# The first group of products behind each norm: high-part products ahead of low-part products, with waits of their own

## The reference, cut to what matters

```python
def rms_norm(x, gain):
    y = x * rsqrt(mean(x * x, axis=-1) + 1e-6)
    return y * gain

h = rms_norm(x, gain)
first = h @ w          # the group of products that this change touches
```

## Time and profile before

| What | Value |
|---|---|
| median of 3 runs | 1635.24 us (1633.99 to 1635.32) |
| profiled execution, device time | 1636.7 us |
| span of its profile | 1634.9 us |
| mean granted TensorE clock | 0.994 |
| DMA | 269.63 MB, mean 165 GB/s |

### The profile page before, as it was taken

The page is one execution under the profiler, slowest core; times in us unless marked ns, Lnnn a source line. Parts: engine busy times, 40 slices in busy tenths (PEclk is TensorE's granted clock), DMA queues, the critical chain, the costliest instruction groups (busy, mean ns, idle before and its releaser), DMA issues. The chain is left out here.

```text
span 1634.9 us, 23336 instructions
## 1 busy us (share of the span) xinstructions
PE 1594.5 (98%) x8942; PEld 1375.3 (84%) x8942; DVE 951.6 (58%) x1449; ACT 801.9 (49%) x1352; POOL 165.8 (10%) x187
## 2 busy tenths in 40 slices
PE   7999999999999999999999999999999999999897
PEld 6888899988888887888889988878888879878886
DVE  5555475444765545555456544665554688577865
ACT  6444464445364444444355454454443555453642
POOL 0000022211200000000021221120000301010100
PEclk9999999999999999999999999999999999999998
DMA  7666455343555555655546443446665453255421
GB/s 244 207 201 203 147 177 192 131 142 129 168 174 186 182 191 166 196 188 184 183 143 197 155 129 127 150 152 213 206 207 192 152 181 117 78 170 170 143 70 52
DMA packets 76431, 269.63 MB, mean 165 GB/s; under 512 B 8480, under 2 KB 9504, under 8 KB 76320
## 3 DMA queue, kind: packets, MB, share of 16 engines
q1 hardware_dynamic: 76320, 268.14, 49.9%
HBM read 267.06 MB, written 1.05 MB: 164 GB/s over the span
## 5 line engine op out<-in xcount | busy, mean ns | idle before, releaser
L289 DVE TENSOR_TENSOR wlo<-raw,whi 128x1024 fp32r<-128x1024 f32 (+4 forms) x468 | 564.9, 1214 | 414.4 <-ACT whi L283 371.2
L283 ACT ACTIVATE whi<-raw 128x1024 fp32r<-128x1024 f32 (+3 forms) x496 | 508.5, 1034 | 433.2 <-PE bank L339 408.3
L337 PE MATMUL bank<-whi,hh 128*128 128x512 f32 (+4 forms) x1312 | 497.8, 379 | 6.8 <-DVE hl L373 3.7
L339 PE MATMUL bank<-whi,hl 128*128 128x512 f32 (+4 forms) x1312 | 486.4, 371 | 0.0
L338 PE MATMUL bank<-wlo,hh 128*128 128x512 f32 (+4 forms) x1312 | 485.8, 370 | 0.0
L337 PEld LDWEIGHTS bank<-whi,hh 128*128 128x128 f32 x1312 | 248.1, 189 | 49.7 <-DVE hl L373 7.0
L339 PEld LDWEIGHTS bank<-whi,hl 128*128 128x128 f32 x1312 | 247.8, 189 | 40.3
L338 PEld LDWEIGHTS bank<-wlo,hh 128*128 128x128 f32 x1312 | 248.3, 189 | 37.3
L337 PE MATMUL bank<-hh,whi 128*128 128x256 f32 x480 | 142.1, 296 | 0.0
L339 PE MATMUL bank<-whi,gl 128*128 128x512 f32 x352 | 138.7, 394 | 0.0
L338 PE MATMUL bank<-wlo,gh 128*128 128x512 f32 x352 | 137.9, 392 | 0.0
(11 more groups left out here) (295 smaller groups left out, 1672.3 us busy)
## 6 DMA issues: line engine op xcount, KB each, us to landing
raw<-W SPq DMA_DIRECT2D x464, 512.0 KB, 3.3
raw<-W SPq DMA_DIRECT2D x26, 384.0 KB, 3.5
raw<-W SPq DMA_DIRECT2D x8, 416.0 KB, 3.0
tab<-tab SPq DMA_DIRECT2D x6, 384.0 KB, 3.9
raw<-W SPq DMA_DIRECT2D x4, 426.0 KB, 3.1
raw<-W SPq DMA_DIRECT2D x6, 192.0 KB, 2.8
x<-x_in SPq DMA_DIRECT2D x2, 512.0 KB, 5.8
tab<-gains SPq DMA_DIRECT2D x2, 512.0 KB, 4.3
```

The lines of the kernel that those rows point to most:

```text
L283: high = act.op(lambda e: e.activation(whi[i][:, 0:w], r[:, 0:w], ACT.Copy), self.landed[c], free)
L289: tok = (low or dve).op(lambda e: e.tensor_tensor(wlo[i][:, 0:w], r[:, 0:w], whi[i][:, 0:w].bitcast(F), ALU.subtract), self.landed[c], hig ...
L337: pe.op(lambda e: e.matmul(dst, ah, bh, start=start, stop=False), *tokens, mark=False)
L339: return pe.op(lambda e: e.matmul(dst, al, bh, start=False, stop=stop), mark=mark)
```

## The change

In a call with a norm, each held chunk is now issued in two passes. The first pass issues, for both k-tiles of the chunk, the two matmuls that read `hh`. The second issues the one that reads `hl`. The first pass waits for the chunk's weights and for a new token, the last ACT operation that wrote `hh` of that half; the second waits for the last `hl`. Number, form and operands of the matmuls stay the same, as do all programs of ACT, DVE, POOL and SP. Only the order of PE's matmuls inside a chunk of these eight groups and PE's waits differ.

```diff
@@ row_group
             k = 0
+            first = norm
             while k < nk:
@@
-                        for kk in range(k0, k0 + n):
+                        if first:
+                            dst, tsl = got[t][1][:, 0:w], slice(t * 128, (t + 1) * 128)
+                            for kk in range(k0, k0 + n):
+                                ws = slice((kk - k0) * w, (kk - k0 + 1) * w)
+                                mm(dst, hh[:, kk, tsl], ch[:, ws], kk == 0, False, ready, first.high[t, kk // 4],
+                                   got[t][2])
+                                mm(dst, hh[:, kk, tsl], cl[:, ws], False, False)
+                            for kk in range(k0, k0 + n):
+                                ws = slice((kk - k0) * w, (kk - k0 + 1) * w)
+                                tok = mm(dst, hl[:, kk, tsl], ch[:, ws], False, kk == nk - 1, first.ready[t, kk // 4],
+                                         mark=(kk == k0 + n - 1))
+                        for kk in range(k0, k0 + n) if not first else ():
                             j = kk - k0
                             tok = mm3(got[t][1][:, 0:w], [p[:, kk, t * 128:(t + 1) * 128] for p in a],
@@
-                hold = 1
+                hold, first = 1, None
                 yield
@@ Norm
+                self.high = {}
@@ Norm.turn
-                self.ready[t, n] = low
+                self.high[t, n], self.ready[t, n] = high, low
```

## The result

| | before | after |
|---|---|---|
| median | 1635.24 us | 1630.98 us (1629.26 to 1632.83, 13 runs) |
| profiled execution, device time | 1636.7 us | 1630.93 us |
| span of its profile | 1634.9 us | 1629.1 us |

The ratio to the kernel before, run beside it, is 0.9971, with a 95% interval of 0.9963 to 0.9980: 4.7 us less (3.3 to 6.0). The forecast was 1629.5 us, 5.7 us less. Direction, mechanism and range were right; the size was 1.0 us too large in the ratio.

The account below looks back on a forecast made before the run. PE, busy 98% of the span, was taken to bound the kernel. Stalls of 5.9 us removed less 0.2 added gave 5.7 us less, from the median 1635.24 to 1629.5 us; range 1627.6 to 1632.9.

Parts of the forecast that it names:

- The bound and the place: PE, busy 98% of the span, bounds the kernel; L337's loads wait for `hl` in eight places, 7.0 us in all.
- The loss per place: At row tile 1's first matmul after eight norms: 0.62, 0.86 and 0.84 us in three places, 5.9 us in all.
- The restart of 0.11: After a stall at 512 columns the next matmul comes 0.34 us behind instead of 0.23, another 0.11 lost.
- What the change adds: A small stall stays in the two first mixers, 0.2 us together; 32 more waits on loads, taken at 0.
- Exactly when `hl` is there: At 416 columns, row tile 1's fifth matmul falls at 207.90; its load wants to begin 0.19 sooner, costing 0 to 0.30.
- The bound of 0.30 each: Upper bound per new wait on a load: bare load of 0.19 plus restart of 0.11, 9.6 us in all.
- Does the gain come through?: Behind each place the weights' chain must keep up; in the first place its slack falls from 3.0 to 2.2 us.
- half of it swallowed: Rival: work begun before the stall (squares, row factor, queued loads) keeps its time, half the gain goes, 1632.4; chance 0.12.
- Nothing happens: Rival: the first pass still waits on DVE behind `hl`, the stall stands, 1635.2; chance 0.04.
- the new waits cost: Rival: each of 32 new waits keeps its load from being hidden, 0.30 each, 9.6 us, giving 1639.1; chance 0.03.
- The clock's stretches: Rival: late phases meet one half-clock stretch more or less, at most 3.4 us, giving 1632.9 or 1626.1; chance 0.06 both ways.
- the seven microseconds of the earlier trace: The 7 us behind 1568, with the clock at 0.51 and 24 PE matmuls, said to cost at most 3.4 us.

Follow-up runs that it names:

- row tile 0 alone: The kernel before, with the two-pass order and split waits for row tile 0 only, row tile 1 issued as before: 1635.70 us, ratio 1.0002.
- the two kernels with one row tile each: The kernel before with the change in one row tile only: row tile 1 gave 1631.25 us, ratio 0.9968; row tile 0 gave 1635.70 us, ratio 1.0002.
- the kernel with the waits alone: The kernel before, its matmul order kept, with the change's split waits: 1635.12 us, ratio 0.9993; run again 1633.18 us, ratio 0.9984.
- the kernel with the order alone: The change's matmul order on the kernel before, the first pass still waiting for `hl`: 1634.96 us, ratio 0.9997.

## Why the prediction was right, and where not

**The bound and the place.** PE is still busy for 98%, and up to 1341 us the path moved by under 0.2 us anywhere else than in the places and at the broadcast. Right.

**The loss per place** (0.62, 0.86 and 0.84 in the three shown, 5.9 in all from one row of the waits). Measured 5.73 won and 2 x 0.10 left, so 5.9. Right to a tenth. The restart of 0.11 was a real part of it: it is 0.9 us of the 5.9.

**What the change adds.** "Exactly when `hl` is there" at 416 columns: the fifth matmul started in its slot and cost the 0.10 that I took. Elsewhere nothing. The 32 new waits were taken at 0. With row tile 0 alone, the twelve within the path cost 0.1 us at most. The bound of 0.30 each was far off.

**Does the gain come through?** This is the step that failed, by 0.64 us. I looked at the weights' chain behind the first place and found 3.0 us of slack, which held: no new wait for weights appeared. I didn't look at the row factor's chain behind each place, which I had named only in a rival. PE itself needs the row factor in four of the eight places, the mixers, where it is broadcast. In three of them PE comes late enough (0.14 us from the first transpose to the next product, before and after). In the seventh place the norm has two gains, `spreads` has a longer chain of small steps, DVE slows them, and PE was already waiting. The mechanism was that of "half of it swallowed": work begun before the stall doesn't move. It took 0.64 of the 5.7, one place whole, not half of all. With it the sum is 5.7 - 0.6 = 5.1 us, and 1630.1 from the median; measured 4.7, interval 3.3 to 6.0, and 1630.98. What is left is smaller than the runs can tell.

**Nothing happens** and **the new waits cost** are excluded by the two kernels with one row tile each, and by the waits table.

**The clock's stretches** did fall otherwise. The price was about right, the framing was not: it is not one stretch more or less behind this change, but three to five in every trace between 1290 and 1610 us, in several patterns, and two traces of one and the same kernel can differ in theirs. Windows of the kernel with the waits alone, and of the kernel before, over the same stretch of time (columns as in the earlier trace rows):

```profile
1388.00:1393.50 5.50, 5.50 (x39) 4.98 (x38) 2.54 (x5) 2.76 (x7) 0.00 (x0) 1.00 0.31 100
1393.50:1397.00 3.50, 3.50 (x14) 3.01 (x14) 1.69 (x8) 0.43 (x2) 0.00 (x0) 0.52 0.00 0
```

```profile
1388.00:1393.50 5.50, 5.50 (x35) 4.75 (x33) 4.99 (x11) 2.62 (x9) 0.00 (x0) 1.00 0.02 4
1393.50:1397.00 3.50, 3.50 (x31) 3.42 (x31) 0.60 (x4) 0.43 (x1) 0.00 (x0) 1.00 0.45 150
```

And the seven microseconds of the earlier trace rows in the kernel with the order alone, whose path is that of before, with a stretch of its own earlier:

```profile
1517.00:1520.40 3.40, 3.40 (x19) 3.40 (x18) 2.91 (x4) 3.38 (x12) 0.00 (x0) 0.50 0.68 233
1568.00:1575.00 7.00, 7.00 (x44) 6.23 (x44) 3.86 (x10) 2.46 (x6) 0.00 (x0) 1.00 0.13 50
```

In the same 7 us PE ran 24 matmuls before and 44 here, and the path moved by 3.2 us, against the 3.4 of the prediction. A stretch of 3.4 us moved it by 1.6 where nothing else held PE up (for instance from -1.98 to -0.32 in the first two fences' stretch). It isn't always so: over the stretch at 1517 us the path of the kernel with the order alone rose from 0.88 to 1.64 us, and by 1530 us it was back at 1.03. Between the profiled executions of before and after the sum came out even: 13.6 us at half clock in both between 1290 and 1610 us, one stretch of 1.6 us more after (at 1428 us) and one more before (at 1568 us). The kernel with the order alone ended 2.2 us ahead of before by the path, though no stall had gone. This is the scatter of the timings, and the reason why a difference of one microsecond can be read in the path and not in the time.

## What to carry to other kernels

Where a sum of products has operands that come ready one after another, order the matmuls by readiness and let each wait for what it reads; the waits alone gave 3.1 us of 5.1 by the path and the order alone nothing. Cost a stall by starts, not by idle time, and add the restart of the first matmul behind it. Then look, place by place, at what the engine meets next that was begun before the stall: that part of the gain stays behind.

## What was not expected of the hardware

POOL's steps on 128x1 took 0.19 to 0.55 us with DVE idle, and 0.9 to 1.4 while DVE subtracted 128x1024 from 128x1024: four of them 4.7 us instead of 1.4, and the row factor 3.3 us late. Not all work of DVE does this: beside its eviction from a bank (L356, 1285.74 to 1286.49 after) POOL's steps still took 0.19. The Trainium skill ("SBUF — State Buffer", section "SBUF: two separate sides") says that VectorE and GpSimd share a pair of ports by an exclusive lock, and that a VectorE operation with two SBUF inputs holds it for its whole length against a GpSimd operation that reads SBUF. The trace agrees: DVE's operations are 1.22 us long and end at 1287.82, 1288.96 and 1290.10, and the first three slow steps end 0.05 us behind them, at 1287.87, 1289.01 and 1290.15. Had the prediction read POOL's rows with this in mind, the late row factor of the seventh place was in the trace of before:

```profile
1290.91 0.55 POOL L365 TENSOR_TENSOR stat<-stat,half 128x1 f32<-128x1 f32 x1
...
1291.16 4.63 DVE L289 TENSOR_TENSOR wlo<-raw,whi 128x1024 fp32r<-128x1024 f32 x4
...
1291.54 2.03 POOL L365 TENSOR_TENSOR stat<-stat 128x1 f32<-128x1 f32 x2
```

There the last step of the row factor ends at 1296.75, and PE's transpose that needs it starts at 1296.81.
